# A two-layer hybrid decoder step: the transposes of the block inverse on VectorE in 32x32 blocks, in place of TensorE transposes and ScalarE copies

## The reference, cut to what matters

```python
kk = jnp.einsum('bhnid,bhnjd->bhnij', kb, kb)
tmat = bb[..., :, None] * kk * d_strict + jnp.eye(chunk, dtype=jnp.float32)
u = lax.linalg.triangular_solve(tmat, bb[..., None] * vb, left_side=True, lower=True)
w = lax.linalg.triangular_solve(tmat, (bb * jnp.exp(G))[..., None] * kb, left_side=True, lower=True)
```

## Time and profile before

| what | value |
|---|---|
| time, median of 3 runs | 1508.19 us (1506.2 to 1508.9) |
| profiled execution, its own time | 1505.52 us |
| its span in the trace | 1503.7 us |
| busy in that span: TensorE / VectorE / ScalarE | 1450.9 / 866.5 / 617.9 us |
| mean granted TensorE clock | 0.989 of full speed |

### The profile page before, as it was taken

One profiled execution on the slowest core, in us unless ns is written; L12 is line 12 of the kernel. 1 busy time (PEld: TensorE's weight loads), 2 busy tenths in 40 slices (PEclk: granted clock), 3 DMA queues, 4 the chain that ended last, 5 costly groups with the idle time before them and its releaser, 6 DMA issues.

```text
span 1503.7 us, 22845 instructions
## 1 busy us (share of the span) xinstructions
PE 1450.9 (96%) x9628; PEld 1410.1 (94%) x9628; DVE 866.5 (58%) x1446; ACT 617.9 (41%) x976; POOL 37.3 (2%) x124
## 2 busy tenths in 40 slices
PE   8999998989998999999999999999899999999997
PEld 8999998879988999999999999998699789999997
DVE  5655434786377665553476554347864766655433
ACT  5443333553323554333354433346433235543432
POOL 0000001010000000000000000010100000000000
PEclk9999999999999999999999999999999999999999
DMA  6544344221114244433435443442211143444342
GB/s 236 207 140 140 125 143 153 85 84 62 57 57 149 99 153 145 144 132 137 154 131 196 141 141 127 152 142 85 85 61 57 57 170 118 141 143 166 125 150 97
DMA packets 49461, 191.24 MB, mean 127 GB/s; under 512 B 6000, under 2 KB 8432, under 8 KB 48848
## 3 DMA queue, kind: packets, MB, share of 16 engines
q1 hardware_dynamic: 48752, 184.66, 35.4%
q0 software_dynamic: 608, 5.12, 0.8%
HBM read 183.33 MB, written 6.43 MB: 126 GB/s over the span
## 4 chain that ended last, share of the span: by engine, by line
PE 87%; DVE 8%; ACT 3%; issue 1%; DMA 1%; SPq 0%; ACTq 0%; DVEq 0%
PE PS L1381 24%; PE PS L1383 23%; PE PS L1382 23%; PE PS L1540 5%; DVE WL L983 2%; DVE CV L1109 2%; PE PS L1421 2%; PE PS L1422 2%; PE PS L1426 2%; PE PS L1538 1%; PE PS L1705 1%; PE PS L1657 1%; ACT WH L722 1%; ACT XH L739 0%; DVE X L1044 0%
## 5 line engine op out<-in xcount | busy, mean ns | idle before, releaser
L1381 PE MATMUL PS<-XH,WH 128*128 128x336 f32 (+1 forms) x1728 | 553.5, 320 | 4.0 <-DVE WL L983 3.0
L1383 PE MATMUL PS<-XH,WL 128*128 128x336 f32 (+1 forms) x1728 | 542.9, 314 | 0.0
L1382 PE MATMUL PS<-XL,WH 128*128 128x336 f32 (+1 forms) x1728 | 542.7, 314 | 0.0
L983 DVE TENSOR_TENSOR WL<-RAW,WH 128x1024 fp32r<-128x1024 f32 (+1 forms) x312 | 398.3, 1301 | 193.4 <-ACT WH L722 193.3
L722 ACT ACTIVATE WH<-RAW 128x1024 fp32r<-128x1024 f32 (+1 forms) x312 | 343.8, 1118 | 203.7 <-DMA RAW<-in_w_down 172.1
L1381 PEld LDWEIGHTS PS<-XH,WH 128*128 128x128 f32 x1728 | 324.6, 188 | 22.8 <-issue 19.7
L1382 PEld LDWEIGHTS PS<-XL,WH 128*128 128x128 f32 x1728 | 324.8, 188 | 0.0
L1383 PEld LDWEIGHTS PS<-XH,WL 128*128 128x128 f32 x1728 | 324.4, 188 | 0.0
L1381 PE MATMUL PS<-HH,WH 128*128 128x336 f32 (+1 forms) x704 | 221.0, 314 | 0.0
L1383 PE MATMUL PS<-HH,WL 128*128 128x336 f32 (+1 forms) x704 | 220.4, 313 | 0.0
L1382 PE MATMUL PS<-HL,WH 128*128 128x336 f32 (+1 forms) x704 | 220.2, 313 | 0.0
(11 more groups left out here) (229 smaller groups left out, 1324.1 us busy)
## 6 DMA issues: line engine op xcount, KB each, us to landing
RAW<-in_w_up SPq DMA_DIRECT2D x176, 512.0 KB, 4.1
RAW<-in_w_down SPq DMA_DIRECT2D x64, 704.0 KB, 4.0
RAW<-in_w_in SPq DMA_DIRECT2D x56, 512.0 KB, 4.2
RAW<-in_w_out SPq DMA_DIRECT2D x16, 512.0 KB, 4.0
SEQ_S<-in_states SPq DMA_DIRECT2D x2, 2048.0 KB, 10.1
out_state_s<-SEQ_S POOLq DMA_DIRECT2D x2, 2048.0 KB, 6.9
X<-in_x SPq DMA_DIRECT2D x8, 168.0 KB, 5.1
out_y<-X SPq DMA_DIRECT2D x4, 320.0 KB, 2.3
```

What stands on the lines that cost most here:

```text
L983: dve.tensor_tensor(WL[slot][:, cols], RAW[slot][:, cols], WH[slot][:, cols].bitcast(F32), ALU.subtract).then_inc(split_lo.sem, 1)
L1381: pe.matmul(out, wh, xh, start=first, stop=False)
L1382: pe.matmul(out, wh, xl, start=False, stop=False)
L1383: return pe.matmul(out, wl, xh, start=False, stop=last)
```

## The change

The `nt` and `mirror` steps leave TensorE and ScalarE. VectorE makes them with its own transpose instruction, which transposes each 32x32 block in place: one instruction of 128x512 (all four heads) from MI to NI for `nt`, one from NI to MI for `mirror` as long as the blocks of the inverse are at most 32 wide (m < 32). For m = 32 the block that lies below the diagonal moves as well as turns, and two instructions of 32 partitions x 4x32 write it. Three more things follow from it. The lags of these steps shrink from two slots to one. `nt` no longer counts as a product, so a slot that held it has room for another. And neither of the two takes a PSUM bank any longer, so the rotation of banks changes. Two semaphores (`turned`, `mirrored`) replace the evacuation counts, and `kt` waits on ScalarE for the last `mirror`, since it writes over NI.

```diff
-NO_PRODUCTS = ("unit", "o_inv", "o_low", "spread", "mirror")
+NO_PRODUCTS = ("unit", "nt", "o_inv", "o_low", "spread", "mirror")
+SQUARE = 32
...
-            after["x", t, m] = [(("nt", t) if m == 2 else ("y", t, m // 2), LAG)]
+            after["x", t, m] = [(("nt", t), 1) if m == 2 else (("y", t, m // 2), LAG)]
             if m < levels[-1]:
                 after["y", t, m] = [(("x", t, m), LAG)]
-                after["mirror", t, m] = [(("y", t, m), LAG)]
+                after["mirror", t, m] = [(("y", t, m), 1)]
             else:
                 after["yt", t, m] = [(("x", t, m), LAG)]
             if m > 2:
-                after["yt" if m == levels[-1] else "y", t, m].append((("mirror", t, m // 2), LAG))
+                after["yt" if m == levels[-1] else "y", t, m].append((("mirror", t, m // 2), 1))
...
 # ScalarE
-                    elif what == "nt":
-                        evacuated(act.activation(NI[:, t, :, :], group(step, layer), ACT.Copy))
-                    elif what == "mirror":
-                        evacuated(act.activation(MI[:, step[1], :, :], group(step, layer), ACT.Copy))
...
                     elif what == "kt":
+                        act.wait_ge(mirrored.sem, mirrored.at(NTH["mirror", t, LEVELS[t][-2]], layer))
...
 # VectorE
+                    elif what == "nt":
+                        dve.wait_ge(pair_set.sem, pair_set.at(NTH["unit", t], layer))
+                        dve.transpose(flat(NI[:, t, :, :]), flat(MI[:, t, :, :])).then_inc(turned.sem, 1)
+                    elif what == "mirror":
+
+                        _, t, m = step
+                        own(("y", t, m), layer)
+                        if m < SQUARE:
+                            ins = dve.transpose(flat(MI[:, t, :, :]), flat(NI[:, t, :, :]))
+                        else:
+                            for low in range(0, P, 2 * SQUARE):
+                                top, bottom = slice(low, low + SQUARE), slice(low + SQUARE, low + 2 * SQUARE)
+                                ins = dve.transpose(MI[top, t, :, bottom], NI[bottom, t, :, top])
+                        ins.then_inc(mirrored.sem, 1)
...
 # TensorE
-                    elif what == "nt":
-                        pe.wait_ge(pair_set.sem, pair_set.at(NTH["unit", t], layer))
-                        per_head_products(step, layer, lambda h: MI[:, t, h, :], None, transpose=True)
                     elif what == "x":
 
                         _, t, m = step
-                        evacuated(("nt", t) if m == 2 else ("y", t, m // 2), layer)
+                        if m == 2:
+                            pe.wait_ge(turned.sem, turned.at(NTH["nt", t], layer))
+                        else:
+                            evacuated(("y", t, m // 2), layer)
```

More of the change, by code:

```diff
@@ L265 @@
 EVACUATED_BY = {
-    "gate_rows": "dve", "cum": "act", "gb": "act", "qk": "dve", "kk": "dve", "vt": "act", "nt": "act", "x": "dve", "y": "dve",
-    "mirror": "act", "yt": "dve", "kt": "act", "kst": "dve", "nv": "dve", "ks": "dve", "o": "act", "st": "dve", "rob": "dve",
+    "gate_rows": "dve", "cum": "act", "gb": "act", "qk": "dve", "kk": "dve", "vt": "act", "x": "dve", "y": "dve",
+    "yt": "dve", "kt": "act", "kst": "dve", "nv": "dve", "ks": "dve", "o": "act", "st": "dve", "rob": "dve",
     "sn": "dve",
@@ L446, in decoder_trunk @@
         dd_raw, dd_exp = sig("dd_raw", TT), sig("dd_exp", TT)
-        pair_set = sig("pair_set", TT)
+        pair_set, turned = sig("pair_set", TT), sig("turned", TT)
+        mirrored = sig("mirrored", sum(len(levels) - 1 for levels in LEVELS.values()))
         filled = sig("filled", len(GROUP_ORDER))
@@ L479, in heads_bank, with flat @@
             return PS[:, 5 + GROUP_INDEX[name] % 3, :].rearrange("p (h n) -> p h n", h=HEADS)
+        def flat(ap):
+            return ap.rearrange("p h n -> p (h n)")
         def blocks(ap, m, parity):
@@ L1548, in mixer, with mirror_made @@
             def mixer(layer):
+                def mirror_made(t, m):
+                    pe.wait_ge(mirrored.sem, mirrored.at(NTH["mirror", t, m], layer))
                 if layer == 0:
@@ L1635, in mixer @@
                         if step[2] > 2:
-                            evacuated(("mirror", t, step[2] // 2), layer)
+                            mirror_made(t, step[2] // 2)
                         per_head_products(step, layer, lambda h: MI[:, t, h, :], lambda h: XB[t][:, h, :])
```

## The result

The changed kernel is slower. Its median is 1526.92 us (4 runs, 1523.89 to 1528.45), beside 1508.55 for the kernel before in the same rounds (4 runs, 1506.20 to 1509.04): ratio 1.0126, 95% interval 1.0114 to 1.0139, so 18.4 us more. The prediction said 1507.5, range 1497 to 1512.5. The profiled execution took 1527.5 us, with a mean granted clock of 0.970 (0.989 before).

What follows compares the result with a forecast made beforehand. TensorE was taken to bound the kernel. Per mixer, -6.5 (transposes) + 2.2 (stage 1) - 0.45 (bank wait) + 4.4 (stage 4) gave about -0.35 us, so 1507.5 us, range 1497 to 1512.5.

Steps and rivals of the forecast that it cites:

- what bounds the kernel: Whole kernel: TensorE, busy 1450.9 of 1503.7 us; work taken off it shortens the kernel unless it must then wait.
- what was removed: TensorE, per mixer: 3 `nt` and 12 `mirror` at 0.43 us come off, 6.5 us.
- the price of a transpose: VectorE: one 128x512 transpose taken at 0.69 us, lower bound 0.45, upper 1.2.
- The rival of the dear transpose: VectorE transposes at 1.2 us each add 2 us per mixer, 1511.5, with 4 more if the stage lengthens; chance 0.12.
- the walk of stage 1: Slots 24 to 29: new TensorE waits 2.5 us at `x_0_2`, 1.1 at `x_1_2`, old 1.4 gone; loss 2.2 per mixer.
- the waits of stage 4: Slot 54 to mixer's end: `sn_1_0` waits 3.5 us, `sn_2_0` 0.7, `sn_3_0` 2.8; the stage costs 4.4 more per mixer.
- The forecast of 59.6 us: Stage 4: time from tile 22's first part to the first `out`, 57.3 before; 2.1 of work is done earlier.
- The clock falls: Slower rival: TensorE's clock drops after the new `sn_1_0` wait, +2 to 2.5 us per mixer, 1512; chance 0.10 including missed waits.
- 2 us lost for one pause: Layer boundary in the old profile: a pause of about 3 us, then TensorE's clock at 0.71 and 0.50, costing 2 us.
- the new wait of 3.5 us at `sn_1_0`: Stage 4, slots 54 on: TensorE waits 3.5 us where it waited 0.83, called the first of that size inside a mixer.
- VectorE's chain, not TensorE, sets the end of this stage: Stage 4: argument against the lower-clock rival, which put +2 to 2.5 us per mixer; chance 0.10 with missed waits.

Runs made afterwards that it cites:

- experiment 1: The changed kernel with the old step order (lags of two slots, `nt` counted as a product), transposes still on VectorE: 1495.27 us, 0.9911 of the kernel before.
- experiment 7: The changed kernel with unused TensorE matmuls filling only the waits ahead of `sn_1_0` and `sn_3_0`: 1509.53 us, 1.0012 of the kernel before.
- experiment 9: The changed kernel with the old step order and `nt` placed directly behind `unit` on VectorE: 1499.82 us, 0.9949 of the kernel before.
- experiments 4: The changed kernel with only `nt` moved directly behind `unit` on VectorE: 1520.67 us, 1.0079 of the kernel before.
- 6: The changed kernel with unused TensorE matmuls filling the waits ahead of `x_0_2`, `sn_1_0` and `sn_3_0`: 1510.12 us, 1.0017 of the kernel before.
- 3: The changed kernel with `o` steps that are a slot's first filler put behind its fixed work (`hi`, `tap`): 1502.92 us, 0.9961 of the kernel before.
- 8: The changed kernel with only the lag from `nt` to `x` back at two slots: 1495.15 us, 0.9916 of the kernel before.

## Why the prediction was wrong

**Right: what bounds the kernel, and what was removed.** 15 x 0.43 = 6.5 us per mixer came off: experiment 1 gained 13.2 us, with the waits for `nt`, `x` and `y` in stage 1 nearly unchanged in sum (2.9 us in the run, 3.1 before).

**Right: the price of a transpose.** 0.70 us measured, 0.69 taken. The rival of the dear transpose is out.

**Right: the walk of stage 1.** `x_0_2` waits 2.37 (2.5). The 1.1 at `x_1_2` looked wrong in the changed kernel, where TensorE at the low clock came late; with the clock kept up it is 1.19.

**Right: the waits of stage 4; its length came out short.** The convolution of slot 54 starts 6.0 us behind tile 22 (419.33 to 425.33; forecast 5.9), with ScalarE's WH behind the copies of `o_0`; the waits are within 0.2 us. The forecast of 59.6 us from there to the first `out` came out as 68.8 (419.33 to 488.13), but as 61.8 where the waits are filled (experiment 7: 418.99 to 480.75), and there the clock still dips once (0.81 from 438 to 446). How much of these 2.2 us per mixer is that dip and how much the walk can't be told from the runs. (Two of the walk's own sums are slightly short: 3.2 + 1.0 + 1.58 is 5.8, not 5.9, and 43.6 + 1.05 + 15.2 is 59.8, not 59.6. Neither matters.) As a sum: the order without the clock costs 1509.5 - 1495.3 = 14.2 us over both mixers, where the walk had 2.2 + 4.4 - 0.45 = 6.15 each, 12.3. By the medians, without the clock the walk would have been 2 us off; the 14.2 still hold the dip.

**Wrong: the term for the clock.** The step that failed is the rival "The clock falls", priced at "+2 to 2.5 per mixer" with "2 us lost for one pause", and given, with any missed wait, 0.10. It measured 17.4 us over both mixers (by the rows of experiment 7, 7.0 in layer 0 and 9.7 in layer 1). That is nearly all of the 19.4 us between the forecast of 1507.5 and 1526.9. Three parts of it failed:

- *How many pauses.* Only "the new wait of 3.5 us at `sn_1_0`" was counted. My own walk had a second one, 2.8 at `sn_3_0`, and the clock fell behind it as well (0.76 from 454 to 462, 0.60 from 462 to 470). The wait of 2.4 in stage 1 lowered the clock too, but cost nothing.
- *How long it stays low.* I took the length of the boundary's stretch. Here it is at 0.50 for some 10 us from `sn_1_0`'s wait on, and at 0.50 to 0.72 from 1200 to 1232 in layer 1.
- *Whether it matters.* I argued that "VectorE's chain, not TensorE, sets the end of this stage". True in stage 1, where experiment 7 shows the lower clock to be free. False in stage 4: there the two engines wait for each other in turn. In the changed kernel VectorE idles for the slow `sn`:

```profile
437.48 1.12 DVE L1319 SCALAR_TENSOR_TENSOR SEQ_S<-SEQ_S,SEQ_EL,PS 128x128 f32<-128x128 f32 x4 [2.18 <-PE PS L1720]
```

In experiment 7 it idles 1.22 us at the same instruction. A walk at full clock can't show that TensorE would become the slower one at half of it.

The Trainium skill ("TensorE: Matmul & The Clock Gate", HAM oscillation — how this bites in real kernels) describes a kernel in which every wait puts the clock down again, so that the price is paid once per wait and not once per kernel. The trace agrees for the long waits: two per mixer at its end (3.29 and 2.67 us), two stretches at 0.50. I had cited the page for the default state and not for this.

**Open.** Why the clock fell behind waits of 0.33 us at `sn_1_0` in experiment 7 (near 437.5, in full work) and 0.82 in experiment 9, and not behind 2.28 in experiment 9; and why `sn_1_0` still waits 2.01 with the `o` steps behind the fixed work. No run was made to settle these.

## What to carry to other kernels

When a walk says that an engine will wait, price each of the waits again at the lower clock: ask what TensorE does behind it, how long that takes at half speed, and whether another engine's lead can absorb it; where the two engines handed work back and forth it couldn't. Shorter lags and freed slots don't have to come with the change that allows them; they are changes of order, to be tried apart from it: here moving the transposes gave 13 us and one lag taken along cost 32. And TensorE's busy time rising while its work falls was here the first sign of a lowered clock; filling the suspected wait with unused matmuls tested it in one run.

## What the hardware showed that I had not expected

- A pause of 2.4 us (`x_0_2`) was followed by a clock of 0.50, while the kernel before, with pauses of 1.10 to 1.76 us in its mixers, shows 1.00 in the windows around them (334 to 358, 470 to 486).
- The length of the pauses doesn't settle it. Early in the mixer every kernel has the same products and the same two waits, 1.27 and 1.51 us. The first row below is from the changed kernel, where the clock stays at 1.00, the second from experiment 7, where it is 0.50 from 306 to 310 and the same matmul takes 0.62 us in place of 0.39. In layer 1 of experiment 7 it stays at 1.00 there. It fell at this place also in layer 0 of experiments 4 and 6 and in layer 1 of experiments 1, 3 and 8. So a single trace that shows 1.00 behind a pause doesn't say that such a pause is safe.

```profile
306.48 0.39 PE L1397 MATMUL PS<-XH,WH 128*128 128x336 f32 x1 [1.51 <-DVE WL L985]
```
```profile
305.34 0.62 PE L1397 MATMUL PS<-XH,WH 128*128 128x336 f32 x1 [1.51 <-DVE WL L985]
```

- The fall can come in the pause or well behind it. Half-microsecond windows of the changed kernel: ahead of `sn_1_0` the clock falls near 434.3, 2.2 us into the idle time; behind `x_0_2`, which starts at 344.41, only near 345.5, in full work.

```profile
434.00:434.50 0.50, 0.00 (x0) 0.00 (x0) 0.50 (x3) 0.00 (x0) 0.00 (x0) 0.77 0.00 0
434.50:435.00 0.50, 0.00 (x0) 0.00 (x0) 0.50 (x2) 0.00 (x0) 0.00 (x0) 0.50 0.00 0
345.00:345.50 0.50, 0.50 (x7) 0.50 (x6) 0.36 (x2) 0.00 (x0) 0.00 (x0) 1.00 0.00 0
345.50:346.00 0.50, 0.50 (x5) 0.50 (x4) 0.39 (x1) 0.00 (x0) 0.00 (x0) 0.52 0.14 33
```

- It stays low although TensorE is busy without a gap: five windows of 2.00 busy out of 2.00 from 436 to 446, four at 0.50 and the last at 0.87.
- 34 unused matmuls per mixer, in place of most of 6 us of idle time, brought back 17 us over two mixers.
- A transpose of 128x512 f32 in 32x32 blocks takes VectorE 0.70 us, as long as its plain copy of the same size from PSUM.
